# Two layer-1 steps moved by one: the low parts of the queries, and the finished outputs of the last pair

## The reference

```python
def mixer_a(h, hc, w_in, sinks, w_o, cos, sin, ctx_out):
    q, k, v, g = jnp.split(h @ w_in, [...], axis=-1)
    q = apply_rope(q...); k = apply_rope(k...)
    kvc = hc @ w_in[:, A_WIDTH:A_WIDTH + 2 * A_KV_WIDTH]
    ...
    s_loc = jnp.where(valid, einsum(qs, ks) * scale, NEG_INF)   # own and neighbouring blocks of 128
    s_ctx = einsum(qs, kc) * scale                              # all context keys
    p = jax.nn.softmax(concatenate([s_loc, s_ctx, sink]))
    o = einsum(p_loc, vs) + einsum(p_ctx, vc)
    y = (o * jax.nn.silu(g)) @ w_o
```

## Time and profile before

| | |
|---|---|
| median of 3 runs | 1149.62 us (1149.59 to 1149.74) |
| the profiled execution | 1151.69 us, its span 1149.9 us |
| busy, share of the span | PE 95%, DVE 57%, ACT 56%, POOL 45% |
| chain that ended last | PE 75%, DVE 12%, ACT 6%, issue 4%, POOL 3% |
| granted TensorE clock, mean | 0.992 of full |

### The profile page before, as it was taken

One profiled execution on the slowest core, in us unless ns is written; L12 is line 12 of the kernel. 1 busy time (PEld: TensorE's weight loads), 2 busy tenths in 40 slices (PEclk: granted clock), 3 DMA queues, 4 the chain that ended last, 5 costly groups with the idle time before them and its releaser, 6 DMA issues.

```text
span 1149.9 us, 19916 instructions
## 1 busy us (share of the span) xinstructions
PE 1093.9 (95%) x7342; PEld 902.4 (78%) x7342; DVE 657.5 (57%) x1305; ACT 647.3 (56%) x1355; POOL 518.9 (45%) x580
## 2 busy tenths in 40 slices
PE   5899999999998899999999999999999999999996
PEld 2688788887885789887788878898787778888785
DVE  7474444455468536254646657735767774527735
ACT  4614555565557418642777768746567653457733
POOL 2733112212110526674899803326644336455871
PEclk9999999999998999999999999999999999999998
DMA  9651232323123311241464634043121404213112
GB/s 374 240 182 47 111 116 55 108 61 124 43 61 123 118 55 38 74 128 55 112 158 99 142 68 72 22 147 106 56 69 55 153 18 144 78 55 128 38 37 74
DMA packets 51724, 113.31 MB, mean 99 GB/s; under 512 B 20452, under 2 KB 23012, under 8 KB 51244
## 3 DMA queue, kind: packets, MB, share of 16 engines
q1 hardware_dynamic: 51628, 112.04, 32.2%
HBM read 105.33 MB, written 2.17 MB: 93 GB/s over the span
## 4 chain that ended last, share of the span: by engine, by line
PE 75%; DVE 12%; ACT 6%; issue 4%; POOL 3%; DMA 0%; DVEq 0%; SPq 0%; POOLq 0%; ACTq 0%
PE PS L707 30%; PE PS L690 15%; PE PS L842 8%; PE PS L830 7%; PE PS L1031 6%; PE PS L1099 3%; PE PS L742 1%; DVE AD L2462 1%; ACT AF L1324 1%; PE PS L723 1%; ACT AR L1604 1%; DVE AF L2159 1%; POOL AR L2643 1%; DVE AR L2363 1%; PE PS L932 1%
## 5 line engine op out<-in xcount | busy, mean ns | idle before, releaser
L2643 POOL TENSOR_TENSOR AR<-AF,AR 128x256 fp32r<-128x256 f32 x396 | 305.9, 805 | 480.1 <-ACT AR L1203 480.1
L707 PE MATMUL PS<-AR 128*128 128x512 f32 (+1 forms) x2208 | 450.7, 360 | 2.9 <-POOL AR L2643 1.4
L707 PEld LDWEIGHTS PS<-AR 128*128 128x128 f32 x2208 | 364.0, 189 | 69.5 <-issue 10.5
L690 PE MATMUL PS<-AR 128*128 128x256 f32 (+4 forms) x1284 | 245.6, 327 | 8.8 <-ACT AF L1324 3.7
L690 PEld LDWEIGHTS PS<-AR 128*128 128x128 f32 (+1 forms) x1284 | 180.6, 190 | 41.6 <-issue 16.5
L1333 ACT ACTIVATE AF<-PS 128x512 f32<-128x512 f32 (+3 forms) x192 | 124.7, 649 | 106.8 <-PE PS L830 101.1
L1324 ACT ACTIVATE AF<-PS,AF 128x512 f32<-128x512 f32 (+3 forms) x192 | 141.1, 735 | 24.8 <-DVE AF L2439 18.3
L2098 DVE CUSTOM_DVE_ANT_0 PS<-PS,AF 128x512 f32<-128x512 f32 (+2 forms) x96 | 68.3, 714 | 119.7 <-PE PS L690 118.9
L830 PE MATMUL PS<-AF 128*128 128x128 f32 x864 | 128.4, 276 | 8.4 <-ACT AF L1333 3.3
L830 PEld LDWEIGHTS PS<-AF 128*128 128x128 f32 x864 | 100.4, 141 | 34.2 <-issue 18.9
L1203 ACT ACTIVATE AR<-AF 128x1024 fp32r<-128x1024 f32 x99 | 103.2, 1051 | 33.6 <-PE PS L1031 27.8
(11 more groups left out here) (231 smaller groups left out, 1214.1 us busy)
## 6 DMA issues: line engine op xcount, KB each, us to landing
AF<-wstream SPq DMA_DIRECT2D x171, 512.0 KB, 4.5
AR<-sums SPq DMA_DIRECT2D x12, 192.0 KB, 3.5
AF<-x_in SPq DMA_DIRECT2D x2, 1024.0 KB, 8.4
AD<-rows SPq DMA_DIRECT2D x4, 512.0 KB, 6.0
out<-AF SPq DMA_DIRECT2D x16, 128.0 KB, 1.9
AF<-AF SPq DMA_DIRECT2D x28, 64.0 KB, 2.0
AF<-rpb_band SPq DMA_DIRECT2D x8, 224.0 KB, 4.5
BIAS<-rpb_band SPq DMA_DIRECT2D x8, 224.0 KB, 5.0
```

What stands on the lines that cost most here:

```text
L690: mm = pe.matmul(out, stationary, moving, start=i == 0, stop=i == len(products) - 1)
L707: mm = pe.matmul(out[:, 0:t1 - t0], a, b, start=k == 0 and i == 0, stop=k == nk - 1 and i == 2)
L2643: ins = pool.tensor_tensor(w[:, 1, at:at + 256], raw(c)[:, at:at + 256], w[:, 0, at:at + 256].bitcast(F32), ALU.subtract)
```

## The change

`split_q` is cut in two. Its two casts stay where they are, in the fifth step of a pair; its two subtractions (L2019) become `split_q_low`, called by `later_a` one step later, in the pair's sixth and last step. Pair 0, which is split before the loop, calls both one after the other as before. `outputs_after` gives each of the last seven steps one output: the first has 0 alone instead of 0 and 1, and the last has 6 instead of none. ScalarE and VectorE both follow that list.

```diff
         def outputs_after(m):
 
-            return [(0, 1), (2,), (3,), (4,), (5,), (6,), ()][m - 6 * (N_PAIR - 1) + 1]
+            return [(0,), (1,), (2,), (3,), (4,), (5,), (6,)][m - 6 * (N_PAIR - 1) + 1]
...
                 for half, h in enumerate(ROWS_OF):
                     ins = dve.tensor_copy(QA[h, p % 2, half, :], QP[h, :])
                 step(ins)
+
+            def split_q_low(p):
+
                 for half, h in enumerate(ROWS_OF):
                     dve.tensor_tensor(QA[ROWS_OF[1 - half], p % 2, half, :], QP[h, :],
                                       QA[h, p % 2, half, :].bitcast(F32), ALU.subtract).then_inc(q_lo, 1)
...
             split_q(0)
+            split_q_low(0)
...
                 elif s == 3:
                     split_q(p)
+                elif s == 4:
+                    split_q_low(p)
```

## The result

| | before | after |
|---|---|---|
| median | 1149.61 us | 1176.28 us (4 runs, 1175.57 to 1178.24) |
| ratio | | 1.0238, 95% interval 1.0226 to 1.0250 |
| profiled execution, span | 1151.69, 1149.9 us | 1178.24, 1176.4 us |
| TensorE's second scores of layer A to its last weighing of values | 286.40 us | 315.37 us |

The kernel became 26.7 us slower. It is taken from the rows of one execution: the start of the first scores (L690) that wait for VectorE, 99.84 us before and 98.55 after, and the start of the last eight matmuls of L842, 386.24 and 413.92. It leaves out the kernel's start: the first scores stand between 97.7 and 100.9 us in the thirteen profiled executions, whatever the edit.

The account below looks back on a forecast made before the run. TensorE, busy 95% of the span, was taken to bound the kernel. Six gaps 18.0, half clock 7.8, seventh boundary 2.3 and outputs -1.6 summed to 26.5 us, added to 1149.6: 1176.1 us, range 1164 to 1185.

Parts of the forecast that it names:

- the stretch behind that gap: First step of the last pair: the slow stretch goes when the gap shrinks to 1.0 us, -1.5 us.
- the last step: Last step: output 6 stands ahead of the turned probabilities on ScalarE, so TensorE waits, +0.9 us.
- The gap: Six equal pair boundaries: TensorE idle 3.4 us, scores late by 3.7 us, 3.4 without GpSimd.
- What comes back: Six equal boundaries: idle time in TensorE's later weight loads disappears, at most 0.7 us each, net 3.0 us per boundary.
- The clock: Behind each of six gaps: one slow stretch at half clock, 1.3 us each, 7.8 us in all.
- Case B: Six boundaries: the clock holds, no slow stretches, 1168.3 us; chance 0.15.
- case C: Six boundaries: each gap brings two slow stretches, 1184 us; chance 0.09.
- The seventh boundary: Before the last pair: TensorE's scores 2.8 us late, 0.5 given back, net 2.3 us, no slow stretch added.
- Part 2: Last seven steps, one output each: first step -2.5 us, last step +0.9 us, net -1.6 us.
- What was to show it: Signs: seven score waits, some 3.4 us, last over 4; clock digits falling at each boundary; pair period about 40.9 us.
- case D: Pair boundaries: half the gap is absorbed, for instance by a hidden wait, 1160 us; chance 0.05.
- case E: Pair boundaries: low parts in by 277.9 us, so TensorE does not wait; faster, 1144.8 us; chance 0.04.

Follow-up runs that it names:

- e3_gap_filled: Changed kernel plus twelve unused 128x512 matmuls on TensorE in each of the seven gaps, ahead of the wait for the low parts: 1165.54 us, ratio 1.0134.
- e2_outputs_only: Kernel before, low parts still directly behind their casts, with only the outputs changed to one in each of the last seven steps: 1150.67 us, ratio 1.0001.
- e6_low_before_gate: Changed kernel with both low parts between the last step's two score reductions, ahead of the gate, instead of at the step's end: 1165.08 us, ratio 1.0125.
- e4_casts_ahead: Changed kernel with casts in step 2 behind the rotation of the queries and low parts back in their old place: 1149.69 us, ratio 0.9998.
- e10_seventh_filled: Kernel before with outputs one per step, plus six unused 128x512 matmuls on TensorE at the seventh boundary alone: 1150.08 us, ratio 1.0001.
- e5_low_twice: Changed kernel with the low parts of pairs 1 to 7 computed twice, the first round waited for: 1200.03 us, ratio 1.0439.
- e7_one_low_each: Changed kernel with one low part left behind its cast and only the other moved a step later: 1166.65 us, ratio 1.0148.
- e9_casts_in_idle: Kernel before with outputs one per step and the last pair's casts moved between its two probability scalings: 1147.97 us, ratio 0.9988.

## Why the prediction was right

The forecast was 1176 us, the time 1176.3. The mechanism is shown: TensorE has no filler ahead of a pair's first scores, waits for the low parts at all seven boundaries, and runs at half clock behind most of these gaps. That the time came within 0.3 us is luck: terms were off by up to 3.4 us and cancelled. In layer A (starts of rows in the profiled executions; the second and third from `e3_gap_filled` against after):

| term | forecast, us | measured, us |
|---|---|---|
| six gaps, less what comes back | 18.0 | 14.6 |
| half clock behind the six | 7.8 | 10.2 |
| seventh boundary, scores late by | 2.8 | 2.8 |
| from there to the last pair's first scores (0.5 back, gap shorter by 1.0) | -1.5 | -0.9 |
| the stretch behind that gap | -1.5 | -0.1 |
| the last step | 0.9 | 2.4 |
| sum | 26.5 | 29.0 |

Term by term:

- **The gap.** Forecast 3.4 us of idle time, measured 3.05. The scores are late by 3.25 us at the first boundary (36.85 against 133.44 - 99.84 = 33.60); I had 3.7, with GpSimd's contention in it, and 3.4 without. The row at 94.8 us has the case in which GpSimd runs first, and the rule names no order; at the boundaries the second low part starts before GpSimd does and is not slowed (1.94 for both). The value without contention was the better one.
- **What comes back.** Forecast 0.7, measured 0.8 (3.25 - 2.45). Net per boundary 2.45 instead of 3.0, 14.6 us for six instead of 18.0.
- **The clock.** Forecast one stretch per gap, 1.3 us each. The price of a stretch was right before the allowance for a part in the gap (1.5; measured 1.55), and the allowance was right only for the second of the six gaps, where 1.1 us of the half clock lay in the gap. The number was not: behind the seven gaps of after stood five single stretches and two double ones. By `e3_gap_filled` the clock's share at the seven boundaries is 11.9 us, 10.2 at six and 1.6 at the seventh, where the kernel before has a stretch too. Case B (the clock holds) and case C (two stretches everywhere) both occur, boundary by boundary.
- **The seventh boundary.** Forecast 2.8 us late; with the gap filled the period that ends there is 1.96 us longer (38.44 against 36.48), and with the 0.8 us that come back behind the sixth gap that is 2.8. A gap of "over 4" is 4.49. The statement that no stretch is added was wrong in this execution: 6.8 us there, 3.4 before. It cost nothing more, for the first 2.5 us of it lay in the gap: from these scores to the next first scores it took 10.63 us, and 10.61 in `e2_outputs_only` with one stretch.
- **Part 2.** Forecast -1.6, measured -0.2 (`e2_outputs_only`). The gap and the wait in the last step were right to 0.1 us. The step that failed is the one that counts the saved half clock in full: of its 1.5 us 0.1 arrived, since TensorE then waited for VectorE. And the forecast did not ask whether the new wait of 0.95 us in the last step brings a stretch of its own. In after it did, 1.57 us; in `e2_outputs_only` it did not.
- **The sum.** Layer A grew by 28.97 us, more than the 26.5 forecast. The profiled execution after has 1.3 us less ahead of layer A and 1.2 us less behind it, which no part of the change touches. Read by the layer, the forecast was short by 2.5 us: 3.4 us too much for six gaps, 2.4 too little for the clock behind them, and 3.5 too hopeful for the last pair. That the whole spans differ by just 26.5 us comes from the parts of the program outside the layer.
- **What was to show it.** The waits and the place of the low parts were as said, the period from the first boundary to the second was 40.56 us (forecast 40.9). The page's clock digits did not fall at each boundary: its slices are 29 us long, and a stretch of 3.4 us in one leaves the digit at 9. Only the slice with the double stretch of the seventh boundary has an 8. The stretches by microsecond show them all.

The claims against case D hold: nothing in the pairs took the gaps back beyond 0.8 us each. For case E the low parts would have to be in by TensorE's last transpose; `e6_low_before_gate` comes within 0.87 us of that, and then pays on the output bank.

## What to carry to other kernels

Before an operation moves a step later, look for the cover of its new place, not of the old one: 1.94 us that were free under a projection cost 4 us under nothing. A gap on TensorE costs nearly its length (2.45 us of 3.05 here) and, as a likely extra, one stretch at half clock (1.55 us) or two, so idle time of 3 us is priced at 4 to 5. A saved stretch is worth its full price only where TensorE alone sets the pace behind it; in the last pair 0.1 to 0.5 us of 1.5 were left of it.

## What the runs showed of the hardware

- **Equal gaps, unequal clock.** In kernels whose gaps agree to 0.01 us, the granted clock behind a gap of 3.05 us stayed full, or was 0.50 for 3.4 or for 6.8 us. Behind 2.07 us all three occurred too, and behind 0.87 + 0.98 us the first two. Behind the last step's wait of 0.95 us, with waits of 0.9 and 0.25 us shortly ahead of it, the clock fell for 3.4 us in five executions (after, `e3_gap_filled`, `e4_casts_ahead`, `e6_low_before_gate`, `e10_seventh_filled`) and stayed full in four (`e2_outputs_only`, `e5_low_twice`, `e7_one_low_each`, `e9_casts_in_idle`). So a forecast for one such gap is a mean with a spread, and one execution's layer time carries 1.5 us of chance. The four runs of after lie within 2.7 us of one another.
- **GpSimd slows what starts beside it.** A low part took 0.95 us when it had started before GpSimd's subtraction, and 1.38 us when GpSimd was running at its start (137.04 in `e5_low_twice`). In the last pair of after VectorE's 128x512 subtraction of an output (L2142) took 0.69 us alone, 0.68 us when it started at 402.59, 0.33 us before GpSimd's operation, and 1.22 us at 408.87, 0.10 us behind the start of the next one. The Trainium skill (GPSIMD Engine Reference, 1. Specifications) has the two engines contend when a VectorE instruction reads two SBUF inputs, as all of these do; the trace agrees. That the order of starting matters is read from these rows alone.
